# Two-stage transformer kernel: modulation panels as 512-column split products in the feed-forward loops, head norm by tokens, embeddings split early

## What is computed

```python
o = rms_norm(o, sub_gain) * (1.0 - lam_init)          # attention 0: one norm over 128 per token and head
h = h + o.reshape(b, s, -1) @ w_o
h = h + conv_gated_ffn(rms_norm(h, ffn_norm[i]), ...)
gate = sigmoid(rms_norm(h, norm_g) @ w_gate)
h = h + (p_i @ w_proj) * gate                         # per-layer embedding
...
mod_x = silu(c) @ w_mod[i] + b_mod[i]                 # i = 0, 1: 1024 -> 3072
mod_c = silu(c_ctx) @ w_mod[i] + b_mod[i]
hx = rms_norm_2(x, norm_g[i]) * (1.0 + sc_x) + sh_x
x = x + g_x * yx
```

## Time and profile before

| | us |
|---|---|
| median of 3 runs (lowest to highest) | 1387.62 (1386.74 to 1389.39) |
| the profiled run, its own time | 1387.44 |
| span of its profile | 1385.7 |
| TensorE busy | 1313.0 |
| VectorE busy | 913.4 |
| ScalarE busy | 683.8 |
| POOL busy | 375.7 |

### The profile page before, as it was taken

One profiled execution on the slowest core, in us unless ns is written; L12 is line 12 of the kernel. 1 busy time (PEld: TensorE's weight loads), 2 busy tenths in 40 slices (PEclk: granted clock), 3 DMA queues, 4 the chain that ended last, 5 costly groups with the idle time before them and its releaser, 6 DMA issues.

```text
span 1385.7 us, 24959 instructions
## 1 busy us (share of the span) xinstructions
PE 1313.0 (95%) x9168; PEld 1146.1 (83%) x9168; DVE 913.4 (66%) x1397; ACT 683.8 (49%) x1207; POOL 375.7 (27%) x390
## 2 busy tenths in 40 slices
PE   6989999999999998999999999999989999999996
PEld 5877899999988886798999999878845588987656
DVE  6868667777767696656777777745257547453674
ACT  5554445555535577634555555434367613422662
POOL 4931135333342050052533333203002311000012
PEclk9999999999999899999999999999999999999998
DMA  8565546655544444074655665222300093633100
GB/s 303 176 236 170 185 137 204 183 181 183 182 128 135 131 145 122 1 289 129 214 183 183 183 183 159 88 92 76 102 21 1 22 246 104 182 101 91 46 1 31
DMA packets 52656, 191.60 MB, mean 138 GB/s; under 512 B 6048, under 2 KB 6304, under 8 KB 52320
## 3 DMA queue, kind: packets, MB, share of 16 engines
q1 hardware_dynamic: 43488, 158.59, 36.6%
q0 software_dynamic: 8368, 31.33, 7.3%
q10 hardware_dynamic: 720, 0.57, 0.1%
HBM read 189.41 MB, written 1.05 MB: 137 GB/s over the span
## 4 chain that ended last, share of the span: by engine, by line
PE 72%; DVE 9%; issue 9%; ACT 7%; POOL 2%; DMA 1%; SPq 0%; DVEq 0%; ACTq 0%; POOLq 0%
PE G L400 12%; PE G L402 12%; PE G L401 12%; PE A L400 6%; PE A L402 6%; PE A L401 6%; PE R L525 3%; PE R L606 3%; DVE WL L1050 2%; ACT WH L1657 2%; PE A L928 1%; PE R L400 1%; PE R L402 1%; PE R L401 1%; DMA RAW<-in_wst 1%
## 5 line engine op out<-in xcount | busy, mean ns | idle before, releaser
L1050 DVE TENSOR_TENSOR WL<-RAW,WH 128x1024 fp32r<-128x1024 f32 x295 | 393.7, 1341 | 304.4 <-ACT WH L1657 303.9
L1657 ACT ACTIVATE WH<-RAW 128x1024 fp32r<-128x1024 f32 x295 | 310.5, 1057 | 433.8 <-PE G L402 310.9
L400 PE MATMUL G<-XH,WH 128*128 128x256 f32 (+1 forms) x1336 | 402.1, 301 | 11.3 <-DVE WL L1050 7.5
L401 PE MATMUL G<-XL,WH 128*128 128x256 f32 (+1 forms) x1336 | 398.2, 298 | 0.0
L402 PE MATMUL G<-XH,WL 128*128 128x256 f32 (+1 forms) x1336 | 398.0, 298 | 0.0
L400 PEld LDWEIGHTS G<-XH,WH 128*128 128x128 f32 x1336 | 256.1, 192 | 22.8 <-issue 11.5
L401 PEld LDWEIGHTS G<-XL,WH 128*128 128x128 f32 x1336 | 256.2, 192 | 7.3
L402 PEld LDWEIGHTS G<-XH,WL 128*128 128x128 f32 x1336 | 256.2, 192 | 7.1
L400 PE MATMUL A<-HH,WH 128*128 128x256 f32 x352 | 99.8, 283 | 0.0
L401 PE MATMUL A<-HL,WH 128*128 128x256 f32 x352 | 99.6, 283 | 0.0
L402 PE MATMUL A<-HH,WL 128*128 128x256 f32 x352 | 99.6, 283 | 0.0
(11 more groups left out here) (339 smaller groups left out, 2412.7 us busy)
## 6 DMA issues: line engine op xcount, KB each, us to landing
RAW<-in_wst SPq DMA_DIRECT2D x295, 512.0 KB, 3.6
M<-in_wmod POOLq DMA_DIRECT2D x48, 512.0 KB, 4.9
B<-in_rpb POOLq DMA_DIRECT2D x4, 1024.0 KB, 20.8
H<-in_x_t SPq DMA_DIRECT2D x2, 512.0 KB, 8.5
M<-in_x_tok SPq DMA_DIRECT2D x1, 1024.0 KB, 13.2
M<-in_ctx_t POOLq DMA_DIRECT2D x1, 1024.0 KB, 5.2
out_y<-M SPq DMA_DIRECT2D x2, 384.0 KB, 2.6
C<-in_cst SPq DMA_DIRECT2D x1, 737.0 KB, 15.6
```

Source lines behind the costliest of these rows:

```text
L400: mm(out, lh, rh, start=start, stop=False, skip_group_check=True)
L401: mm(out, lh, rl, start=False, stop=False, skip_group_check=True)
L1050: v.tensor_tensor(WL[:, slot, :], RAW[:, raw, :], WH[:, slot, :].bitcast(F32), ALU.subtract).then_inc(w_lo, 1)
L1657: act(WH[:, slot, :], RAW[:, raw, :], ACT.Copy).then_inc(w_hi, 1)
```

## The change

- Only 16 of the 48 modulation panels (PLAIN) stay as fills: 12 products before attention 0, 5 a step in it, and 14 + 6 + 6 in the head norm.
- The other 32 are laid out as 128 rows of 2 x 512 columns (8 of them make 512 output columns) and are done inside the feed-forward loops, 16 in each. POOL's queue brings them (`gathers`), ScalarE and VectorE split them (`high`, `rest`) into a part of XH and XL; `refill` multiplies them, after a tile, with four columns that hold c and c_ctx split into high and low part (SCR): four products of 512 columns a panel. Four panels add up in O to one row block, which ScalarE copies to YR (`row`). In `ple` 16 small products with SEL add the two halves and turn them (`turn_gathered`).
- The head norm works with tokens as rows: the values are multiplied the other way round (OTOK), POOL squares each head as it comes, VectorE sums over channels and scales, in two groups of four heads of which the first lies within the attention; TensorE turns the result, and the gain goes into the copy out of PSUM.
- The embedding is split early, behind the second tile of the loop, into XH[8:10] and XL[8:10]; in `ple` ScalarE makes the squares of H and POOL only adds them; all fills there are gone.
- All later fills, and the turns and copies that belonged to them, are gone.

```diff
-FILLED = 32
-HELD = 44
-PERO = 16
+PLAIN = 16
+GROUPS = 4
...
+            def refill(layer, s, i):
+                if s == 0:
+                    pe.wait_ge(r_y, i + (2 + 5 * layer))
+                pe.wait_ge(r_lo, i * 4 + (5 + PLAIN * layer + s))
+                for c in range(2):
+                    for w in (RH, RL):
+                        m = mm(O[0:32, :], SCR[:, 2 * s + c, :], w[:, 512 * c:512 * c + 512],
+                               start=(s == 0 and c == 0 and w is RH), stop=(s == 3 and c == 1 and w is RL),
+                               skip_group_check=True)
+                m.then_inc(m_used, 1)
...
+            def turn_gathered(layer):
+                pe.wait_ge(r_y, 1 + 5 * (layer + 1))
+                for t in range(PLAIN):
+                    m = mm(O[:, 2 * t:2 * t + 2], YR[0:4, 512 + t * P:512 + (t + 1) * P], SEL, start=True, stop=True,
+                           skip_group_check=True)
+                m.then_inc(m_tr, 1)
...
+            def heads_turn(g):
+                for tt in range(2):
+                    pe.wait_ge(hn_ok, 2 * g + tt + 1)
+                    for i in range(4):
+                        m = nc.tensor.transpose(A[2 * g + tt][:, i * P:(i + 1) * P],
+                                                OTOK[:, tt, (4 * g + i) * P:(4 * g + i + 1) * P], IDT)
+                    m.then_inc(hn_tr, 1)
...
+            fill(12)
             pe.wait_ge(bias_ok, 1)
-            attention("l0", scores_l0, value_l0, 6)
-            for c in range(4):
-                fill(5)
-                head_stat(HN["l0_o"] + c, ONES)
-            fill(48)
+            attention("l0", scores_l0, value_l0, 5)
+            fill(14)
+            heads_turn(0)
+            fill(6)
+            heads_turn(1)
+            fill(6)
             for u in range(4):
-                gemm_unit(U0["l0_o"] + u, START["l0_o"] + 2 * u, 0, KD, 8, 2, fresh=XS["l0_o"] if u == 0 else None)
-            turn_modulators(0, A[0])
+                gemm_unit(U0["l0_o"] + u, START["l0_o"] + 2 * u, 0, KD, 8, 2,
+                          fresh=[XS["l0_o"] - 4] * 4 + [XS["l0_o"]] * 4 if u == 0 else None)
+            turn_modulators(A[0])
...
-                                if fresh is not None and k == 6:
-                                    fill(8)
...
-                for d in range(2):
-                    q = p0 + 4 + 3 * d
-                    fill(4)
-                    if layer == 0 and d == 0:
-                        pe.wait_ge(m_ok, 1)
-                    hidden(d, q, (u0 + d) % 2, (u0 + 2 + d) // 2, q)
-                    down(d, q + 2, hb + 1 + d, q + 2, d == 0, False)
-                with pe.Fori(0, 9) as i:
-                    for d in range(2):
-                        q = p0 + 10 + 3 * d
-                        hidden(d, q, (u0 + d) % 2, (u0 + 4 + d) // 2 + i, q + 6 * i)
-                        down(d, q + 2, hb + 3 + d + 2 * i, q + 2 + 6 * i, False, False)
+                def tile(j, i=0, filled=None):
+                    q = p0 + 4 + 3 * (j - 2)
+                    hidden(j % 2, q, (u0 + j) % 2, i * 2 + (u0 + j) // 2, i * 12 + q)
+                    down(j % 2, q + 2, i * 4 + (hb + j - 1), i * 12 + (q + 2), j == 2, False)
+                    if filled is not None:
+                        refill(layer, filled, i)
+                if layer == 0:
+                    pe.wait_ge(m_ok, 1)
+                for j in range(2, 7):
+                    tile(j)
+                with pe.Fori(0, 3) as i:
+                    for d in range(4):
+                        tile(7 + d, i, d)
+                for d in range(3):
+                    tile(19 + d)
+                    refill(layer, d, 3)
                 down(0, p0 + 64, hb + FT - 1, p0 + 64, False, False)
-                fill(8)
+                refill(layer, 3, 3)
                 down(1, p0 + 65, hb + FT, p0 + 65, False, True)
...
-                fill(24)
                 pe.wait_ge(p_hi, layer + 1)
                 pe.wait_ge(p_lo, layer + 1)
                 for u in range(4):
-                    gemm_unit(U0[a] + u, START[a] + u // 2, 4 * (u % 2), 2, 0, 2, xh=HH, xl=HL)
-                    if u % 2:
-                        fill(8)
+                    gemm_unit(U0[a] + u, START[a] + u // 2, 4 * (u % 2), 2, 8, 2)
+                turn_gathered(layer)
                 for u in range(4):
-                    gemm_unit(U0[b] + u, START[b] + 2 * u, 0, KD, 8 - 8 * layer, 2, fresh=XS[b] if u == 0 else None)
+                    gemm_unit(U0[b] + u, START[b] + 2 * u, 0, KD, GATE[layer], 2, fresh=XS[b] if u == 0 else None)
                     if u == 0:
...
-            fill(FILLED * KD - fills[0])
...
-                if u == 2:
-                    turn_modulators(1, O)
...
-            fill(8)
             context_ahead()
             pe.wait_ge(row_rt, RSW["ac"][2] + 1)
             row_stats("a")
-            fill(HELD * KD - fills[0])
...
-            wide_unit(0, XS["a"], None, lambda: turn_modulators(2, O))
+            wide_unit(0, XS["a"], None, None)
...
             row_stats("b")
-            fill(MODS * KD - fills[0])
...
+            def heads_summed(g):
+                dv.wait_ge(hn_sq, 4 * g + 4)
+                v.tensor_reduce(token_sum(g, 8), HRS[:, :, :].rearrange("p a (h d) -> p (a h) d", h=4), AX,
+                                ALU.add).then_inc(hn_ss, 1)
+            def heads_applied(g):
+                sc = token_scale(g, 8)
+                dv.wait_ge(hn_rt, g + 1)
+                v.reciprocal(sc, sc).then_inc(hn_rc, 1)
+                dv.wait_ge(hn_rc, g + 1)
+                for tt in range(2):
+                    o = OTOK[:, tt, 512 * g:512 * g + 512].rearrange("p (h d) -> p h d", h=4)
+                    v.tensor_tensor(o, o, sc[:, 4 * tt:4 * tt + 4].unsqueeze(2).broadcast_to([P, 4, P]),
+                                    ALU.mult).then_inc(hn_ok, 1)
+            def heads_rest(g):
+                for tt in range(2):
+                    xn[0] += 2
+                    dv.wait_ge(x_hi, xn[0])
+                    t = slice(tt * P, (tt + 1) * P)
+                    v.scalar_tensor_tensor(XL[:, 8 + 4 * g:12 + 4 * g, t], A[2 * g + tt].rearrange("p (k t) -> p k t", k=4), SUBG,
+                                           XH[:, 8 + 4 * g:12 + 4 * g, t].bitcast(F32), ALU.mult,
+                                           ALU.subtract).then_inc(x_lo, 2)
+            attention("l0", bias_l0, None, 0, 16)
+            heads_summed(0)
+            attention("l0", bias_l0, None, 16)
+            heads_applied(0)
+            heads_summed(1)
+            heads_applied(1)
+            heads_rest(0)
+            heads_rest(1)
...
+                dv.wait_ge(p_hi, layer + 1)
+                v.tensor_tensor(XL[:, 8:10, :], PIN[:, layer, :, :], XH[:, 8:10, :].bitcast(F32), ALU.subtract).then_inc(p_lo, 1)
+                def rest(s, i):
+                    dv.wait_ge(r_hi, i * 4 + (PLAIN * layer + s + 1))
+                    v.tensor_tensor(RL, RR[:, s, :], RH.bitcast(F32), ALU.subtract).then_inc(r_lo, 1)
+                for j in range(2, 6):
+                    p = p0 + 4 + 3 * (j - 2)
+                    turn(j % 2, (u0 + j) % 2, j, p, p + 3, p + 3, hb + j)
+                with dv.Fori(0, GROUPS) as i:
+                    for d in range(4):
+                        p = p0 + 16 + 3 * d
+                        turn(d % 2, (u0 + d) % 2, i * 4 + (6 + d), i * 12 + p, p + 3, p + 3, i * 4 + (hb + 6 + d))
+                        rest(d, i)
...
+            def heads_root(g):
+                ac.wait_ge(hn_ss, g + 1)
+                act(token_scale(g, 8), token_sum(g, 8), ACT.Sqrt, bias=EPSC, scale=1.0 / P).then_inc(hn_rt, 1)
+            def heads_out(g):
+                for tt in range(2):
+                    ac.wait_ge(hn_tr, 2 * g + tt + 1)
+                    act(XH[:, 8 + 4 * g:12 + 4 * g, tt * P:(tt + 1) * P], A[2 * g + tt].rearrange("p (k t) -> p k t", k=4),
+                        ACT.Copy, scale=SUBG).then_inc(x_hi, 2)
+            attention("l0", out_l0, 0, 18)
+            heads_root(0)
+            attention("l0", out_l0, 18)
+            heads_out(0)
+            heads_root(1)
+            heads_out(1)
+            rows_out()
...
+                act(XH[:, 8:10, :], PIN[:, layer, :, :], ACT.Copy).then_inc(p_hi, 1)
...
+                def high(s, i):
+                    ac.wait_ge(r_raw[s], i * 16 + (64 * layer + 16))
+                    ac.wait_ge(m_used, i * 4 + (PLAIN * (layer + 1) + s))
+                    act(RH, RR[:, s, :], ACT.Copy).then_inc(r_hi, 1)
+                def row(i, used):
+                    ac.wait_ge(m_used, used)
+                    act(YR[:, bass.ds(i * 512, 512)], O[0:32, :], ACT.Copy).then_inc(r_y, 1)
+                for j in range(2, 6):
+                    p = p0 + 4 + 3 * (j - 2)
+                    turn(j % 2, (u0 + j) % 2, (u0 + j) // 2 + 1, j, p, p + 3, lands(p), hb + j)
+                with ac.Fori(0, GROUPS) as i:
+                    for d in range(4):
```

(56 more changed lines are left out.)

231 lines of the change are left out of this document (95 added, 136 removed).

## The result

| | time, us (median, range) | against the kernel before | mean clock |
|---|---|---|---|
| before | 1387.18 (1386.34 to 1389.39) | | 0.989 |
| after | 1396.22 (1392.69 to 1397.47) | 1.0059, 95% interval 1.0036 to 1.0081 | 0.977 to 0.979 |

The changed kernel is slower by 0.6%. The forecast was 1391.8 with a range of 1380 to 1400, and "slower" was the likeliest sign. Against the kernel before the median is 9.0 us longer where the forecast said 4.4.

What follows compares the result with a forecast made beforehand. The prediction took TensorE, busy for 95% of the span and never idle in the feed-forward loops, as the bound. Its gains, refill costs and clock losses summed to +4.4 us on 1387.44, giving 1391.8, range 1380 to 1400.

Steps and rivals of the forecast that it cites:

- The loops: Feed-forward loops: 14 of 16 refills a layer cost TensorE 0.92 us each, +12.9 a layer; two hide at the end.
- Attention 0: Fewer fills, but POOL's squares slow VectorE: 1.0 us gained, plus 1.3 from the clock at its start, together -2.3.
- Head norm: Last value product to output projection, 19.8 us made by four reciprocals in a row, becomes 8.8 us: -11.1.
- Loop starts: Feed-forward loop starts: removing fills gains 0, moved embedding copy costs +0.7 a layer; clock gaps add 1.0 + 0.7 and 1.3 + 0.7.
- Embeddings: Last down product to first gate product in each layer: fills and wait go, -9.5 and -4.9; gathered products take 3.6 us.
- Start of layer 1: Removed fills gain 0, removed turn and copies 0.7; idle time grows from 1.3 to 3.9 us, clock costs 2.0.
- Gate units: Gate units of both layers, behind the gathered products: forecast 0, no clock loss listed there.
- Mixer a: Start of mixer a: earlier row sums and removed VectorE wait give -4.0; the clock behind a 6.1 us gap costs 2.2.
- The clock: Half clock behind new gaps at layer 1's start, mixers a and b and both loop starts: +10.1 in sum.
- Rival 2: Slower through the half clock: 2.7 us at seven places, thin work not bringing the clock back, 1400.6; chance 0.08.
- Rival 1: Faster: only three long gaps drop, gathered products cost 2 us, attention gives 4.1: 1380.2; chance 0.36 with its half version.
- Rival 3: Slower through VectorE: shared-port and ScalarE waits lengthen loop tiles, 0.5 us over 28 tiles, 1406; chance 0.06.

Runs made afterwards that it cites:

- Experiment 3: The kernel before with 84 of the 112 fills in its waits left out: 1396.26 us, ratio 1.0056 to the kernel before.
- 5: The changed kernel with one 512-column product per refill instead of four: 1379.95 us, ratio 0.9946 to the kernel before.
- experiment 2: The changed kernel with useless 128x128 products on TensorE ahead of the emptied waits: 1389.54 us, ratio 1.0006 to the kernel before.
- experiment 6: The changed kernel with the added splits cut to 32 of 1024 columns on ScalarE and VectorE: 1393.4 us, ratio 1.0039 to the kernel before.
- Experiment 8: The kernel before with the four head norm reciprocals over 32 columns of 512: 1387.3 us, ratio 0.9994 to the kernel before.
- experiment 1: The changed kernel run once more without edit: 1394.94 us, ratio 1.0049 to the kernel before.
- experiment 4: The changed kernel with 1 gathered product instead of 16 in each layer: 1388.8 us, ratio 1.0006 to the kernel before.
- combo: The changed kernel with useless products in waits, gathered products spread over gate units, last four panels as plain products in mixer b's wait: 1379.71 us, ratio 0.9943.
- warm_all: The same run as experiment 2, the changed kernel with useless products ahead of the emptied waits: 1389.54 us.
- embed_late: The changed kernel with the layer embedding's copy and rest back behind the feed-forward loop: 1404.92 us, ratio 1.0133 to the kernel before.

## Why the prediction was right, and where it was not

**The mechanism held, the places of the clock in part by luck.** The change takes fills out of places where they were hidden and puts refills into the one place where TensorE has no idle time; the stretches that shrink (head norm, embeddings) pay for the refills almost exactly; the clock behind the emptied waits decides the sign. Experiment 3 shows the first step (84 fills fewer gain nothing), 5 the second, 3 and 2 the last.

**The loops** were forecast at +12.9 a layer and measured +13.5. The product costs 0.23 us as taken. The 0.6 us is in the two small waits at the loop's end: refills 3 and 4 "cost nothing" because the last tile's chain ends late anyway, but the added splits on VectorE and ScalarE made that very chain some 0.8 us later, which experiment 6 takes back. The term that was missing is the effect of new work on VectorE on the wait that was to hide TensorE's.

**Attention 0** gained 4.6 us for 2.3. The step that failed is the price of the squares on POOL: I let VectorE become the bound of a pair of steps. The bound that I wrote down for hidden squares (all 18 fills, 4.1 us, gained) was nearer: up to the first turn of probabilities the stretch is 2.2 us shorter, of which three fills are 0.7 and the clock 1.5 (forecast 1.3), which leaves about 3 of the 4.1. Six of the eight squares took 0.60 or 0.61 us, less than the 0.74 that I had taken. By the Trainium skill ("SBUF — State Buffer", SBUF: two separate sides) the loser of the shared port waits for the whole instruction. The trace agrees in that one of the two loses, but not in the size, 0.4 us beside a square of 0.60, and here VectorE lost although its instruction is recorded 0.05 us before the square; the kernel as a whole doesn't notice.

**Head norm** came out as forecast, -10.9 for -11.1, though its text puts it down to "four reciprocals of 3.35 us in a row". Experiment 8 shows that these alone are worth under 1 us. The sum was right because it counted the fills and transposes that remain as well, and they, not the reciprocals, made its 8.8 us.

**Loop starts.** The +0.7 for the moved copy of the embedding did not show, and of the two gaps "near the edge" at each start the second is always absorbed: behind a slow stretch of 24 products the next wait is shorter by as much (0.95 for the 2.36 us that experiment 2 laid bare). Layer 0 cost 0.4 for 2.4, layer 1 1.8 for 2.7.

**Embeddings**: -9.3 and -4.7 for -9.5 and -4.9. The 32 gathered records took 3.77 us, the upper end of what I had considered (3.6). The nearest row, 128 rows deep, had 0.115 us a record and this one, four rows deep, 0.118. The Trainium skill ("TensorE: Matmul & The Clock Gate", LDWEIGHTS (loading the stationary operand)) says that a weight load goes by its columns; by this pair of rows the trace agrees.

**Start of layer 1.** The stage was forecast at +1.3 and measured +1.1, and that is luck. Instead of one wait of 3.9 us there are three, 0.90, 1.36 and 2.39 us. The clock falls behind the last, but the start had its low stretches in the kernel before as well: the sum over 2-us windows is 5.1 us there in both kernels. From the end of the first gate unit to the products at 465 us (475 in the kernel before) the changed kernel even gains 0.4 us, for a forecast of 0.7 gained and 2.0 lost. What the stage lost was in attention 1, some 1.7 us behind the untouched wait of 1.91 us, and experiment 1 has the full clock there.

**Gate units.** The step that was missing altogether. I asked of each idle time whether it would cost the clock, and never of each stretch of work. The gathered products are busy time of 100% in every view and 2.9 us were lost behind them (7.43 and 7.51 us for twice 6.0); experiment 4 gives them back.

**Mixer a** was forecast at -4.0 + 2.2 and measured +0.3. The idle 1.99 us of the earlier trace rows went, as foreseen, and the last gate unit ran at full clock. But the context products ahead now wait three times for their splits (0.58, 1.36 and 0.72 us where the kernel before had none behind its 8 fills), so the row sums did not come earlier; and the clock took 2.5 (60 products of 512 columns in 16.3 us, at 0.23 each 13.8).

**The clock** as a sum was about right: forecast +10.1, and in the profiled run 0.4, 2.9 (gate units), 1.8 (layer 1), 1.8, 2.5 and 1.9 (mixers a and b), 11.3 in all (the 1.8 of layer 1 in its attention), less 1.4 where the last gate unit of layer 1 no longer ran slow. The places were partly others than I listed: at those that I had listed it was about 6.6 us (none at the start of layer 1), and the gate units and attention 1, where I had none, made up for it. So the fit of this sum is luck, and part of the closeness of the total (5.2 us for 4.4) with it. Rival 2, with thin work that doesn't bring the clock back, named a mechanism close to what the gathered products do, at 2.7 us a place; measured were 1.4 and 1.5. Rival 1 failed on all of its three conditions: more gaps than the three long ones dropped, the gathered products cost 3.77, and in attention some 3 of the 4.1 us came. Rival 3 is refuted by experiment 6.

**Median against profile.** The forecast was made against one execution and met one; the median is 3.5 us above it. The mean clock of the three other executions is 0.977 for 0.979, and 0.002 of 1391 us is 2.8 us. With experiment 1, where the same gaps drop or keep the clock by turns, the likeliest cause is that more of the gaps of about 2 us dropped in those; no profile of a slower execution exists, so this is argued and not shown.

## What to carry over

Before filler work is taken out of an engine that is idle there anyway, ask what it did for the clock: 84 products fewer made this kernel 8 us slower, and 116 useless ones more made the changed one 6 us faster. Real work belongs there first (the plain products in mixer b), cheaper forms of it only where the engine is never idle. And where a chain and the work beside it are nearly tied, price both; shortening the chain alone gave under 1 us here.

## What the runs showed of the hardware

- TensorE's clock fell to 1.2 GHz behind 3.7 us of gapless two-column products with four-row weights (0.54 and 0.57 in the windows behind), and stayed at 2.4 GHz when the same products came in pieces of 0.6 to 1.3 us between units of 256-column products (1.00 in combo). In warm_all it fell within 32 two-column products with 128-row weights (1.00, then 0.62), with no idle time but 0.28 us.
- An idle time of 1.9 to 2.3 us is followed by the low clock in one execution and not in the next of the same kernel (2.19 us: 1.00 and 0.73; 1.91 us: 0.61 and 1.00). Of two waits of 3.22 us in one execution of embed_late one was followed by 0.64, the other by 1.00.
- Useless 128-column products kept the clock as well as real ones: 1.00 after 24 of them where it had been 0.50 after 6.1 us of idle time.
- A split of 1024 columns on VectorE cost 1.72 us on average in the refills and 1.40 for the weights in the same loop; I have no run that tells why.
